# Stick-breaking attention with a running product, and recurrence scores on half the columns, in a three-block f32 kernel

## What is computed

```
def stick_breaking_attention(q, k, v):            # per head; t = query, s = key
    z = q . k * scale
    mask = s_pos < t_pos
    log_keep = where(mask, log_sigmoid(-z), 0)
    later = cumsum(log_keep, keys, reverse) - log_keep
    w = where(mask, exp(log_sigmoid(z) + later), 0)
    out = w @ v

def hgrn2(q, f_pre, i, lb):                       # chunks of 64 tokens
    b = cumsum(log_f) within the chunk
    scores[t, s] = sum_k q[t, k] k[s, k] exp(b[t, k] - b[s, k])   for s <= t
    o = (q exp(b)) @ state + scores @ i
```

## Time and profile before

| | us |
|---|---|
| median of 3 timed executions | 1050.41 |
| lowest, highest | 1049.27, 1051.16 |
| the profiled execution, device time | 1049.21 |
| its span, first to last instruction | 1047.5 |
| mean granted TensorE clock | 0.989 |
| PE busy | 995.0 (95%) |
| DVE busy | 705.5 (67%) |
| ACT busy | 570.2 (54%) |
| POOL busy | 135.7 (13%) |

### The profile page before, as it was taken

How to read it: one execution, slowest core, us unless ns; L and a number is a source line. 1 busy time by engine, 2 the same in 40 slices (tenths; PEclk the granted TensorE clock), 3 DMA queues, 4 the chain that set the end, 5 groups by cost and what they waited for, 6 DMA issues and landing times.

```text
span 1047.5 us, 16427 instructions
## 1 busy us (share of the span) xinstructions
PE 995.0 (95%) x6658; PEld 909.1 (87%) x6658; DVE 705.5 (67%) x1011; ACT 570.2 (54%) x800; POOL 135.7 (13%) x124
## 2 busy tenths in 40 slices
PE   6998798999999989989899999999999999999996
PEld 6987687999998878777899998888988889999995
DVE  5787755888883574965788888456564566954654
ACT  6735544666563385676565665346574466443432
POOL 4002511243320000000023332000100000000000
PEclk9999998999999999999999999999999999999999
DMA  9553215786656563414676664665645553465541
GB/s 319 178 176 106 81 41 135 206 255 197 186 165 227 183 227 124 148 55 121 174 199 174 188 183 168 212 201 161 203 156 161 161 158 125 160 197 168 201 141 41
DMA packets 165643, 174.38 MB, mean 166 GB/s; under 512 B 4094, under 2 KB 132592, under 8 KB 165568
## 3 DMA queue, kind: packets, MB, share of 16 engines
q1 hardware_dynamic: 163376, 167.92, 51.2%
q0 software_dynamic: 2160, 5.41, 1.7%
q10 hardware_dynamic: 32, 0.01, 0.0%
HBM read 172.25 MB, written 1.07 MB: 165 GB/s over the span
## 4 chain that ended last, share of the span: by engine, by line
PE 74%; ACT 9%; DVE 9%; issue 5%; DMA 2%; POOL 1%; SPq 0%; POOLq 0%; ACTq 0%; DVEq 0%
PE bank L811 36%; PE bank L792 18%; PE bank L830 12%; PE bank L846 4%; ACT w_hi L1143 3%; DVE w_lo L1446 2%; DMA w_raw<-in_ab_w_in 2%; PE bank L875 1%; ACT le_s L1371 1%; ACT le L1242 1%; DVE prod L1523 1%; POOL sp__80 L659 1%; ACT L1242 0%; DVE ex L1500 0%; DVE exb L1500 0%
## 5 line engine op out<-in xcount | busy, mean ns | idle before, releaser
L1446 DVE TENSOR_TENSOR w_lo<-w_raw,w_hi 128x2048 fp32r<-128x2048 f32 x157 | 358.7, 2289 | 186.7 <-ACT w_hi L1143 186.7
L1143 ACT ACTIVATE w_hi<-w_raw 128x2048 fp32r<-128x2048 f32 x157 | 299.8, 1914 | 259.1 <-PE bank L811 146.0
L811 PE MATMUL bank<-x_hi,w_hi 128*128 128x256 f32 x912 | 260.1, 285 | 2.9 <-issue 2.6
L811 PE MATMUL bank<-x_lo,w_hi 128*128 128x256 f32 x912 | 258.0, 283 | 0.0
L811 PE MATMUL bank<-x_hi,w_lo 128*128 128x256 f32 x912 | 258.0, 283 | 0.0
L811 PEld LDWEIGHTS bank<-x_hi,w_hi 128*128 128x128 f32 x912 | 174.9, 192 | 4.3 <-issue 3.3
L811 PEld LDWEIGHTS bank<-x_lo,w_hi 128*128 128x128 f32 x912 | 175.0, 192 | 0.2
L811 PEld LDWEIGHTS bank<-x_hi,w_lo 128*128 128x128 f32 x912 | 174.9, 192 | 0.0
L792 PE MATMUL bank<-w_hi,x_hi 128*128 128x512 f32 x256 | 102.9, 402 | 8.2 <-issue 4.0
L811 PE MATMUL bank<-y_hi,w_hi 128*128 128x256 f32 x352 | 99.6, 283 | 3.9 <-issue 3.9
L668 POOL TENSOR_TENSOR gf<-sgate,cc 128x256 f32<-128x256 f32 x44 | 82.1, 1866 | 162.0 <-ACT sgate L1164 161.9
(11 more groups left out here) (339 smaller groups left out, 1586.7 us busy)
## 6 DMA issues: line engine op xcount, KB each, us to landing
w_raw<-in_ffn_up SPq DMA_DIRECT2D x88, 512.0 KB, 5.2
w_raw<-in_w_in SPq DMA_DIRECT2D x35, 1024.0 KB, 5.3
w_raw<-in_ffn_down SPq DMA_DIRECT2D x22, 1024.0 KB, 5.0
w_raw<-in_ab_w_in SPq DMA_DIRECT2D x14, 1024.0 KB, 5.3
w_raw<-in_ple_gate SPq DMA_DIRECT2D x8, 1024.0 KB, 5.1
w_raw<-in_c_w_in SPq DMA_DIRECT2D x6, 1024.0 KB, 5.2
w_raw<-in_ab_w_out SPq DMA_DIRECT2D x4, 1024.0 KB, 5.1
w_raw<-in_w_mem_kv SPq DMA_DIRECT2D x4, 1024.0 KB, 5.4
```

The source lines that it names most:

```text
L811: mm = pe.matmul(bank[b][:, c * 256:c * 256 + 256], wv[w][:, k, c * P:(c + 1) * P], x[:, k, :], start=(k == 0 and m == 0 and not (first an ...
L1143: act.activation(whi[n % RING][:, :], raw[n % RAW][:, :], ACT.Copy).then_inc(*mark("weights_hi", ("hi", n)))
L1446: dve.tensor_tensor(wlo[n % RING][:, :], raw[n % RAW][:, :], plain(whi[n % RING][:, :]), ALU.subtract).then_inc(*mark("weights_lo", ("lo", ...
```

## The change

In `shape_constants` the triangular matrix becomes an additive mask (-1e30 on and above the diagonal). The stick-breaking scores are made the other way round, with queries on partitions, and the mask is added in PSUM by a matmul with the identity; the two constants are first rounded to fp32r by ACT (`ident_r`, `tri_r`) in the setup. ACT takes Sigmoid twice from PSUM instead of Abs and Copy. DVE forms the running product over later keys by a scan, POOL multiplies, PE turns the weights, and ACT and DVE copy one head each back to SBUF. These steps (`sb_weights`, `sb_turn`) now stand inside the loop over panels, and `sb_log` is gone. Of the recurrence, `hg_level` is cut in two (`hg_decays`, `hg_factors`), the matmul of a level moves only the later halves (64 columns for each of 8 blocks, one bank), mask and sum have half as many instructions, and the diagonal is done first instead of last. The norm of the recurrence's heads takes its inverse root by one power on POOL instead of a chain of small DVE instructions.

```diff
     for n, li in enumerate(range(-1, 6)):
         out.append(("hg_scores", li))
+        if li < 0:
+            out.append(("hg_scores", DIAGONAL))
+        out.append(("hg_mask", li))
+        if li < 0:
+            out.append(("hg_mask", DIAGONAL))
+        if LEVELS[li + 2]:
+            out.append(("hg_decays", li + 2))
+        if 1 <= n < 5:
+            out.append(("sb_scores", n - 1))
         if 2 <= n < 6:
-            out.append(("sb_scores", n - 2))
-        out.append(("hg_mask", li))
+            out.append(("sb_weights", n - 2))
         if LEVELS[li + 2]:
-            out.append(("hg_level", li + 2))
-        else:
-            out.append(("sb_log",))
+            out.append(("hg_factors", li + 2))
+        if n >= 3:
+            out.append(("sb_turn", n - 3))
         out.append(("panel", first + 3 + n))
-    out.extend([("hg_scores", 6), ("hg_scores", 7), ("hg_mask", 6), ("hg_mask", 7), ("sb_weights", 0), ("sb_weights", 1)])
-    out.extend([("sb_weights", 2), ("hg_out",), ("sb_weights", 3)])
+    out.extend([("hg_scores", 6), ("hg_mask", 6), ("hg_out",)])
...
+        ident_r, tri_r = g("ident_r", [P, P], F32R), g("tri_r", [P, P], F32R)
...
+                elif kind == "hg_norm":
+                    pool.wait_ge(*at(("hgms",)))
+                    pool.tensor_tensor(hg_rs, hg_ss, minus_half[:, 0:1].to_broadcast([P, 8]), ALU.pow).then_inc(*mark("rstd", ("hgrs",)))
                 elif kind == "sb_weights":
                     i = args[0]
-                    pool.wait_ge(*at(("w", i)))
-                    for r in range(2):
-                        earlier_only(zs, 2 * i + r, "weights_masked", ("wm", i))
+                    pool.wait_ge(*at(("past", i)))
+                    pool.wait_ge(*at(("taken", 2 * i + 1)))
+                    c = slice(2 * i, 2 * i + 2)
+                    for t, (at0, n) in enumerate(((0, P), (P, T))):
+                        w = take[:, c, at0:at0 + n]
+                        pool.tensor_tensor(w, w, past[:, :, at0 + t + 1:at0 + t + 1 + n], ALU.mult).then_inc(*mark("sb_weights", ("sbw", i)))
...
+                    else:
+                        pe.wait_ge(*at(("xs", li)))
+                        X, b = xs_buf[li % 2], level_bank(li)
+                        claim(b, ("prod", li))
+                        for hd in range(HG_HEADS):
+                            for t in range(TT):
+                                o = (2 * hd + t) * 64
+                                mm = pe.matmul(bank[b][:, o:o + 64], X[:, hd, t * P:(t + 1) * P],
+                                               later(X[:, hd:hd + 1, t * P:(t + 1) * P], LEVELS[li])[:, 0, :, :], start=True, stop=True)
+                        mm.then_inc(*mark("scores", ("ps", li)))
...
-                        claim(b, ("z", hd))
-                        pe.matmul(bank[b][:, 0:T], kaT[q, i, 0:P], qaT[q, i, :], start=True, stop=True)
-                        mm = pe.matmul(bank[b][:, T:T + P], kaT[q, i, P:T], qaT[q, i, P:T], start=True, stop=True)
+                        claim(b, ("taken", hd))
+                        pe.matmul(bank[b][:, P:2 * P], qaT[q, i, P:T], kaT[q, i, 0:P], start=True, stop=True)
+                        for t in range(TT):
+                            out, c = bank[b][:, 2 * P * t:2 * P * t + P], slice(t * P, (t + 1) * P)
+                            pe.matmul(out, qaT[q, i, c], kaT[q, i, c], start=True, stop=False)
+                            mm = pe.matmul(out, ident_r[:, :], tri_r[:, :], start=False, stop=True)
                         mm.then_inc(*mark("scores", ("sbz", hd)))
-                elif kind == "sb_weights":
+                elif kind == "sb_turn":
                     i = args[0]
+                    pe.wait_ge(*at(("sbw", i)))
                     for r in range(2):
                         hd = 2 * i + r
+                        claim(4 + r, ("sbt", hd))
+                        three_blocks(4 + r, [take[:, hd, 0:P], take[:, hd, P:2 * P], take[:, hd, 2 * P:3 * P]]).then_inc(*mark("turned", ("tr", "sbw", hd)))
...
+                    act.wait_ge(*at(("loaded", "tri")))
+                    act.activation(ident_r[:, :], ident[:, :], ACT.Copy).then_inc(*mark("vectors", ("masks_rounded",)))
+                    act.activation(tri_r[:, :], tri[:, :], ACT.Copy).then_inc(*mark("vectors", ("masks_rounded",)))
...
-                        act.activation(sp_[:, hd, :], bank[b][:, 0:384], ACT.Abs).then_inc(*mark("sb_scores", ("az0", hd)))
-                        act.activation(zs[:, hd, :], bank[b][:, 0:384], ACT.Copy).then_inc(*mark("sb_scores", ("z", hd)))
+                        act.activation(keep[:, hd, :], bank[4 + r][:, 0:384], ACT.Sigmoid, scale=-1.0).then_inc(*mark("sb_gates", ("kept", hd)))
+                        act.activation(take[:, hd, :], bank[4 + r][:, 0:384], ACT.Sigmoid).then_inc(*mark("sb_gates", ("taken", hd)))
+                elif kind == "sb_turn":
+                    i = args[0]
+                    act.wait_ge(*at(("tr", "sbw", 2 * i)))
+                    act.activation(turned[:, 2 * i, :], bank[4][:, 0:384], ACT.Copy).then_inc(*mark("turned_copied", ("sbt", 2 * i)))
...
+                half = LEVELS[li]
+                mask = later(masks[:, li:li + 1, :], half).to_broadcast([P, HG_HEADS * TT, 64 // half, half])
+                dve.tensor_tensor(level_prod(li), bank[level_bank(li)][:, :].rearrange("p (b n c) -> p b n c", b=HG_HEADS * TT, c=half), mask, ALU.mult).then_inc(*mark("masked_scores", ("prod", li)))
...
+                elif kind == "sb_weights":
+                    i = args[0]
+                    dve.wait_ge(*at(("past",)))
+                    if i:
+                        dve.wait_ge(*at(("sbw", i - 1)))
+                    for r in range(2):
+                        hd = 2 * i + r
+                        dve.wait_ge(*at(("kept", hd)))
+                        for t, (at0, n) in enumerate(((0, P), (P, T))):
+                            dve.tensor_tensor_scan(past[:, r, at0 + t:at0 + t + n][:, ::-1], keep[:, hd, at0:at0 + n][:, ::-1],
+                                                   ones[:, 0:1].to_broadcast([P, n]), 1.0, ALU.mult, ALU.mult).then_inc(*mark("sb_products", ("past", i)))
+                elif kind == "sb_turn":
+                    i = args[0]
+                    dve.wait_ge(*at(("tr", "sbw", 2 * i + 1)))
+                    dve.tensor_copy(turned[:, 2 * i + 1, :], bank[5][:, 0:384]).then_inc(*mark("turned_copied2", ("sbt", 2 * i + 1)))
```

More of the change, by code:

```diff
@@ L30 @@
 LEVELS = [64, 32, 16, 8, 4, 2, 1, 0]
+DIAGONAL = len(LEVELS) - 1
 RAW, RING = 3, 3
@@ L1295, in _ @@
                     act.activation(ex[:, :, :], bdec[:, :, :], ACT.Ln).then_inc(*mark("levels", ("logf",)))
[L1296 removed]
+                elif kind == "hg_decays":
                     li = args[0]
[L1298 to L1301 removed]
+                    e = ex if li % 2 == 0 else exb
+                    act.wait_ge(*at(("dd", li)))
+                    act.activation(e[:, :, :], e[:, :, :], ACT.Exp).then_inc(*mark("levels", ("ex", li)))
                 elif kind == "sb_scores":
@@ L1330, in _ @@
                               ("tr", "hg", j), ("pe", last_of("gb")))
-                elif kind == "sb_weights":
-                    i = args[0]
-                    act.wait_ge(*at(("d", 2 * i + 1)))
-                    c = slice(2 * i, 2 * i + 2)
-                    act.activation(zs[:, c, :], zs[:, c, :], ACT.Exp).then_inc(*mark("sb_weights", ("w", i)))
                 elif kind == "sb_out":
```

254 lines of the change are left out of this document (110 added, 144 removed).

## The result

The changed kernel takes 1070.32 us (median of 4 runs, 1068.86 to 1071.21) against 1049.84 us for the kernel before beside it: a ratio of 1.0192, 95% interval 1.0174 to 1.0210. That is 20.5 us slower, where the forecast said 14 (1064 us, range 1056 to 1073). The profiled execution has a span of 1069.4 us and a mean granted clock of 0.974; before it was 1047.5 us and 0.989.

A forecast was written before the change was run, and what follows sets the result against it. Rounds were bound by the loop DVE, Exp, `w_hi`, DVE, with PE keeping up. Rounds and constants +21.4, clock +4.2, tail -11.6 gave +14.0 us on 1049.2: 1063.2, with the median's 1.2 us forecast as 1064, range 1056 to 1073.

The forecast's parts named there:

- Constants: Ahead of the rounds, ACT rounds two constants of 128 columns in a chain DVE waits for: +0.4 us.
- n = 0: First round between starts of `w_lo`: gets the diagonal's two masks from the tail, 8.2 us against 7.0.
- n = 5: Last round: no scores or sigmoids, DVE is the bound, 9.4 us as before.
- n = 1: Second round: ACT's table load and four sigmoids come between Exp and `w_hi`, 11.0 us against 7.6.
- n = 2: Third round: the same as n = 1 with the copies of `ib`, 1.1 us: 12.1 us.
- n = 3 and 4: Rounds where transposes and panel wait for the sigmoids through shared banks: 17.2 and 17.7 us, plus 2.1 each for clock.
- Tail: From the last `w_lo` to the first panel of `wo0`: 16.0 us against 27.6, so -11.6 us.
- Operations not in the trace of before: Assumed prices: level matmul 1.4 us, mask 0.6, scan of a pair 1.9, POOL's product 1.9.
- rival 3: Masks of 64-column pieces are slowed by short runs: 1069 us in total, chance 0.16.
- Rival 4: An ACT table switch costs more than its load, 4 by 1.3 us: 1069 us in total, chance 0.07.

The follow-up runs named there:

- experiment 3: The changed kernel without the mask products in the stick-breaking scores, so keys are not masked: 1065.93 us, ratio 1.0160.
- experiment 6: As experiment 5, with stick-breaking scores and sigmoids behind the panel too and the transposes in banks 2 and 3: 1037.21 us, ratio 0.9873.
- experiment 10: The changed kernel, order kept, with transposes in banks 2 and 3 and level scores in banks 0 and 1: 1055.61 us, ratio 1.0061.
- experiment 8: The changed kernel with 14 unused products of 512 columns ahead of the transposes in rounds 3 and 4: 1066.16 us, ratio 1.0150.
- 11: As experiment 6, but with mask and score products alternating again: 1038.56 us, ratio 0.9896.
- 12: As experiment 6, with the products of `sb_out` ahead of those of `hg_out` in the tail: 1034.86 us, ratio 0.9856.
- experiment 5: The changed kernel with the transposes behind the panel and the mask products together ahead of the score products: 1050.13 us, ratio 0.9991.
- experiment 2: The changed kernel with a pair's four mask products together ahead of its six score products: 1066.56 us, ratio 1.0160.
- experiment 9: The changed kernel run once more, unedited; its profile is the second profile: 1068.68 us, ratio 1.0180.

## Why the prediction was right, and where it wasn't

The side, the mechanism and the range held; the middle was 6 us low. That the range held is in part luck: its upper end came from a slower mask, 5 us, which did not come, and that room took up what the forecast lacked in round 1 and the tail. By its own steps, against the profiled execution (+21.9 us of span, forecast +14.0):

- **Constants, n = 0, n = 5**: 0.35, 8.22 and 9.07 us, forecast 0.4, 8.2 and 9.4. Right.
- **n = 1**: 15.47 us (13.89 in the second profile), forecast 11.0. This is the step that failed most. The prediction counted ACT's chain and didn't ask what the scores wait for at their new place. They stand one round earlier than before, right behind the last panel of `ka`, and `kaT` comes from DVE, queued behind the factors that wait for Exp. DVE's timeline:

```profile
66.15 0.68 DVE L1522 TENSOR_TENSOR xs<-exb,qf 128x512 f32<-128x512 f32 x1
66.75 0.68 DVE L1608 TENSOR_TENSOR kaT<-bank,row_early 128x512 f32<-128x512 f32 x1
```

  PE stands 2.8 us, and then runs the scores (5.2 us) and most of the panel (8.0) at the half clock. An estimate from these rows puts the price on the clock and not on the waiting: at the full clock scores (3.2) and panel (5.5) from 67.54 would end at 76.2 us, no later than the last sigmoid (76.5), and the round would take the forecast 11.0 or so. With the scores 3 us cheaper at the half clock the round took 11.5 (experiment 3), and with the scores behind the panel 8.1 (experiment 6).
- **n = 2**: 14.06 us in the first profile, 12.21 in the second, forecast 12.1. The chain on ACT was right; the rest is the clock.
- **n = 3 and 4**: 18.51 and 19.92 us (18.68 and 20.03), forecast 17.2 and 17.7 with 2.1 each for the clock, 19.3 and 19.8. Right within 0.8 us: experiment 10 shows the shared banks as the cause, experiment 8 the 2.1 us of clock in round 4. In round 3 transposes and panel took 1.58 and 6.32 us where 0.82 and 5.5 are the full clock's, an estimate of 1.6 us; and there the forecast's reason, that the idle PE costs its clock, does not fit the first profile, in which the clock fell before the stand began. The stands were 5.8 and 5.7 us (7.6 and 5.7 in the second profile) where 11 and 8 were forecast, since PE's own scores take 5.0 us and not 3, and in the first profile panel n = 2 came late. The stand's length is not what the rounds pay; the chain through ACT is, and it was read rightly.
- **Tail**: 19.2 us, forecast 16.0. Two terms were mis-sized, both by the clock: panel gb1 took 7.1 us (145.7 to 152.8) behind a stand of 2.7 us for POOL's product, and `hg_out` 4.5 us where 2.8 was set, behind the stand for mask and sum. The level scores took 1.89 us and not 1.4. The forecast put a clock loss on two of the stands and none on those of the tail.
- **Operations not in the trace of before**: scans 1.89 us for a pair (forecast 1.9), masks 0.68 with runs down to one element (0.6; rival 3 falls), exponents 0.68 and 1.76 (0.60 and 1.80). POOL's product took 2.63 us beside DVE's factors and 1.9 was forecast. The level scores with 64 columns took 1.89 of "between half and all of 1.95": all.
- **Rival 4**: a table load takes 1.28 us and the sigmoid starts 0.01 us after it (103.16, 104.45). It falls. The Trainium skill (ScalarE: Activation LUTs, What ACT_TABLE_LOAD costs) puts such a switch at about 2.66 us with a drain of about 1.38; the measurement decides, and these rows leave no room for one.

By parts: recurrence -8.9 us; stick-breaking about +28, of which the shared banks are 14 (experiment 10). What is left goes into the first scores' place, the sigmoids ahead of `w_hi` and the clock, which only the orders of experiments 6, 11 and 12 take away together.

On the level scores, the rows say that halving the moving columns saves 0.06 us in sixteen instructions, 0.118 us each. The Trainium skill (TensorE: Matmul & The Clock Gate, LDWEIGHTS (loading the stationary operand)) makes the time of a weight load go by the load's own columns, by its formula some 0.107 us for 128, an estimate. Each of these products loads 128 columns, and 0.118 us is near that; that the load is what bounds them is not shown by a run.

## What to carry to other kernels

When a step is put at a new place, ask of each of its operands when it is ready there and who is queued ahead of its producer, not only what the step costs. When two steps share a bank, a wait of one engine for another's reader can tie three engines into one chain; giving them banks of their own was worth 14 us here without moving a single instruction. A slow engine's new work (table loads, sigmoids) belongs behind the product that others wait for: the same instructions cost nothing behind `w_hi`, and rounds 2 and 3 with them ahead of it took 3.0 and 2.1 us more (experiment 5 against 6, in which the scores moved with them).

## What the runs showed of the hardware

- Ten small products on PE took 3.2 us when float32 scores and float32r masks alternated, 1.8 us with the four masks together (experiment 2), and the six scores alone 1.3 us (experiment 3). So a mask product costs 0.1 us in company and 0.5 us alone.
- One program showed round 2 at a clock of 0.76 and of 1.00 in two executions, 14.06 and 12.21 us. A clock seen in one profile is not a property of the edit until a second one shows it. The Trainium skill (TensorE: Matmul & The Clock Gate, What's actually happening) says that what the gate watches is free-running and does not start anew with a kernel, so that the point of a change varies; these two profiles agree, in that the same program differs between them.
- The clock's price depends on what is behind the stand: 2.1 us for a stand before a panel in the chain (experiment 8), and nothing where it falls into idle time: in round 3 the clock was low for 11 us in experiment 9 and for 3.5 us in experiment 8, and the round took 18.7 and 18.8 us.
